# Second half of the gated values taken ahead of the last weight units, in the tail of an expert item

## The chip, the cores and the metric

The kernel runs on one core of a Trainium2 chip. The metric is device microseconds (us) for one execution of the whole kernel, as the median of several runs. Engines: PE is TensorE (matmuls and transposes), PEld its weight loads, DVE is VectorE, ACT is ScalarE, POOL is GpSimd, SP is SyncE, which issues the weight transfers.

## The reference, cut to what matters

The layer mixes a short convolution, differential attention and memory attention for 1024 tokens of width 1024, and then runs a mixture of 32 experts of which each token takes 4. Only the experts' part matters here:

```
def expert_block(args):
    tok, g, e = args
    xb = h_pad[tok]
    gu = xb @ w_gate_up[e] + b_gate_up[e]
    gate, up = jnp.split(gu, 2, axis=-1)
    gate = jnp.minimum(gate, SWIGLU_LIMIT)
    up = jnp.clip(up, -SWIGLU_LIMIT, SWIGLU_LIMIT)
    act = (up + 1.0) * (gate * jax.nn.sigmoid(SWIGLU_ALPHA * gate))
    y = act @ w_down[e] + b_down[e]
    return y * g[:, None].astype(y.dtype)
```

## The kernel before

**Items.** The experts' part is a loop over items. An item is one expert with up to 256 of its tokens, in one or two blocks of up to 128. A second block of at most 64 tokens is "short". An item with one block is called single here, one with two double. `by_size` picks the variant of the code by the item's own size, and `size_next` tells whether a next item follows and whether it is double.

**Units.** Each item takes 12 weight units of 1 MB (128 x 2048 floats), numbered u0 to u11: u0 to u3 gate and up for the first 512 columns (c = 0), u4 to u7 the same for the second 512 (c = 1), u8 to u11 the down projection: u8 and u9 with the first half of the gated values a, u10 and u11 with the second half. PE needs a high part and a low part of every operand, since a product is made of three: high x high, high x low, low x high. ACT makes the high part of a unit (`high_unit`, line 1150: a rounding copy), DVE the low part (`low_unit`, line 1564: original minus high). There are four places for high parts, so unit u is rounded once PE has used unit u - 4, and for the first units of the next item this reaches over the end of the item: unit 1 of the next item waits for u9, unit 2 for u10.

**Activations.** The gated values of half c are made on DVE (`products`), turned by PE (`turn_a`, transposes on line 922), rounded by ACT (`a_high`, line 1198) and subtracted by DVE (`a_low`, line 1585). u10 and u11 wait for `a_low` of half 1. The rows of the next item take the same way: `turn_x(b)` on PE (line 915) for block b, `x_high(b)` on ACT (line 1160), `x_low(b)` on DVE (line 1575). Both blocks are turned through the same PSUM banks, so `turn_x(1)`, which exists only before a double item, waits until `x_low(0)` has read them. u0 of the next item waits for `x_low` of all its blocks.

**Results.** ACT copies the down products out (`results`, line 1211, and line 1213 for the lower rows of a short block); for a short block DVE adds and scales (lines 1592 and 1632). Each half of the result raises `y_made`. The second block of the next item's u0 writes a PSUM bank that these results are read from, so in a double item its bias matmul waits for `y_made`:

```
if (len(kinds), b, c) in ((2, 1, 0), (1, 0, 1)):
    pe.wait_ge(s["y_made"], it * 2 + 1)
```

**Order.** Every engine works through its own instructions in the order in which `item` writes them for that engine; nothing reorders them. Across engines there are only semaphores. The order of the tail, from u8 on, is what the change edits.

Of the kernel before, what the change touches and what calls it, by code (L numbers as in the profile page):

```python
# [52 lines left out]
SLOTS = 12  # L53
# [33 lines left out]
def hymba_kernel(nc, a, out):  # L87
    ctx = ExitStack()
    with ctx:
# [596 lines left out]
        def _(pe):  # L686
# [19 lines left out]
            for g in range(NG):  # L706
                u, kind, x, half = groups[g]
# [217 lines left out]
            def use_unit(it, u, kinds):  # L925

                side, c, half = UNITS[u]
                high = w_high_part(u).rearrange("p (k n) -> p k n", k=4)
                low = w_low_part(u).rearrange("p (k n) -> p k n", k=4)
                rows = a_split if side == "d" else x_split  # L930
                pe.wait_ge(s["w_low_made"], it * 12 + (u + 1))
                if side == "d":
                    pe.wait_ge(s["a_low"], it * 2 + (half + 1))
                elif u == 0:
                    for b in range(len(kinds)):
                        pe.wait_ge(s_xlow[b], it + 1)
                    pe.wait_ge(s["picked"], it + 1)
                for b, kind in enumerate(kinds):
                    bank = ps[:, out_bank(side, c, b, kinds), :]
                    if half == 0:  # L940
                        if side == "d":
                            if b == 0:
                                pe.wait_ge(s["y_made"], it * 2 + 1)
                            else:
                                pe.wait_ge(s["silu_made"] if c == 0 else s["up_read"], it * 2 + 3)
                        else:
                            pe.wait_ge(s["silu_made"] if side == "g" else s["up_read"], it * 2 + (c + 1 if len(kinds) > 1 else 1))
                            if (len(kinds), b, c) in ((2, 1, 0), (1, 0, 1)):
                                pe.wait_ge(s["y_made"], it * 2 + 1)
                        which = 1 if side == "d" else 0  # L950
                        row = picked[:, which, 0:P] if kind == "full" else picked[:, which, SHORT:SHORT + P]
                        at = (D if side == "u" else 0) + HALF * c
                        mm(bank, row, mem_r[:, at:at + HALF], True, False)
                    for kk in range(4):
                        k = 4 * half + kk
                        first, second = rows[:, k, b, 0, :], rows[:, k, b, 1, :]
                        mm(bank, first, high[:, kk, :], False, False)
                        last = mm(bank, first, low[:, kk, :], False, kind == "short" and k == KD - 1)
                        if kind == "full":
                            last = mm(bank, second, high[:, kk, :], False, k == KD - 1)  # L960
                last.then_inc(s["w_used"], 1)

            def item(it, size_next, kinds):
                for u in range(6):
                    use_unit(it, u, kinds)

                pe.wait_ge(s["a_made"], it * 2 + 2)
                for b in range(len(kinds)):
                    pe.wait_ge(s_xlow[b], it + 1)
                turn_a(0, kinds)  # L970
                for u in range(6, 8):
                    use_unit(it, u, kinds)
                with pe.If(size_next > 0):
                    pe.wait_ge(s_gather[0], it * 16 + 32)
                    pe.wait_ge(s["a_low"], it * 2 + 1)
                    turn_x(0)
                use_unit(it, 8, kinds)
                pe.wait_ge(s["a_made"], it * 2 + 3)
                turn_a(1, kinds)
                use_unit(it, 9, kinds)  # L980
                with pe.If(size_next > P + 1):
                    pe.wait_ge(s_gather[1], it * 16 + 32)
                    pe.wait_ge(s_xlow[0], it + 2)
                    turn_x(1)
                with pe.Else():
                    pe.sem_inc(s_xturned[1], 1)
                for u in range(10, SLOTS):
                    use_unit(it, u, kinds)

            for b in range(BLOCKS):  # L990
                pe.wait_ge(s_gather[b], 16)
# [4 lines left out]
            with pe.Fori(0, MAX_ITEMS // GROUP) as group:  # L996
                size_group = pe.value_load(table[2:3, bass.ds(group * GROUP + 1, 1)], min_val=0, max_val=CAP + 1)
                with pe.If(size_group > 0):
                    with pe.Fori(0, GROUP) as place_in:
                        it = group * GROUP + place_in  # L1000
# [8 lines left out]
        def _(act):  # L1009
# [136 lines left out]
            def high_unit(it, u):  # L1146

                act.wait_ge(s_w[home(u)], arrived(u, it))
                act.wait_ge(s["w_used"], it * 12 + (u + 1))
                act.activation(w_high_part(u), ring[:, home(u), :], ACT.Copy).then_inc(s["w_high_made"], 1)  # L1150
# [20 lines left out]
            def up_rest(it, c, kinds):  # L1171
                if "short" in kinds:
                    b = kinds.index("short")
                    act.wait_ge(s["w_used"], it * 12 + (HI_SLOTS + 4 * c + 4))
                    act.wait_ge(s["a_turned"], it * 2 + (c + 1))
                    act.activation(up_b[0:SHORT, b, :], ps[SHORT:P, out_bank("u", c, b, kinds), :], ACT.Copy).then_inc(s["rest_made"], 1)
# [39 lines left out]
            def item(it, size_next, kinds):  # L1216
                high_unit(it, 3)
                high_unit(it, 4)
                gate_rest(it, 0, kinds)
                high_unit(it, 5)  # L1220
                sigmoids(it, 0, kinds)
                high_unit(it, 6)
                up_rest(it, 0, kinds)
                high_unit(it, 7)
                gate_rest(it, 1, kinds)
                sigmoids(it, 1, kinds)
                a_high(it, 0, kinds)
                high_unit(it, 8)
                high_unit(it, 9)
                up_rest(it, 1, kinds)  # L1230
                with act.If(size_next > 0):
                    x_high(0, it + 1, "full")
                high_unit(it, 10)
                high_unit(it, 11)
                a_high(it, 1, kinds)
                with act.If(size_next > 0):
                    high_unit(it + 1, 0)
                    expert = act.value_load(table[0:1, bass.ds(it + 2, 1)], min_val=0, max_val=EXPERTS - 1)
                    act.wait_ge(s["w_used"], it * 12 + (HI_SLOTS + 10))
                    pick_expert(bass.ds(expert, 1))  # L1240
                    by_second(act, size_next, lambda kind: x_high(1, it + 1, kind), lambda: act.sem_inc(s_xhigh[1], 1))
                    high_unit(it + 1, 1)
                    high_unit(it + 1, 2)
                for c in range(2):
                    results(it, c, kinds)
                if "short" not in kinds:
                    act.sem_inc(s["rest_made"], 6)
# [34 lines left out]
        def _(dve):  # L1282
# [278 lines left out]
            def low_unit(it, u):  # L1561

                dve.wait_ge(s["w_high_made"], it * 12 + (u + 1))
                dve.tensor_tensor(w_low_part(u), ring[:, home(u), :], w_high_part(u).bitcast(f32), ALU.subtract)\  # L1564
                    .then_inc(s["w_low_made"], 1)
# [68 lines left out]
            def item(it, size_next, kinds):  # L1634
                low_unit(it, 3)
                gates(it, 0, kinds)
                low_unit(it, 4)
                low_unit(it, 5)
                products(it, 0, kinds)
                low_unit(it, 6)  # L1640
                low_unit(it, 7)
                gates(it, 1, kinds)
                a_low(it, 0, kinds)
                low_unit(it, 8)
                products(it, 1, kinds)
                low_unit(it, 9)
                with dve.If(size_next > 0):
                    x_low(0, it + 1, "full")
                with dve.Else():
                    dve.sem_inc(s_xlow[0], 1)  # L1650
                low_unit(it, 10)
                a_low(it, 1, kinds)
                low_unit(it, 11)
                with dve.If(size_next > 0):
                    low_unit(it + 1, 0)
                    by_second(dve, size_next, lambda kind: x_low(1, it + 1, kind), lambda: dve.sem_inc(s_xlow[1], 1))
                    low_unit(it + 1, 1)
                    low_unit(it + 1, 2)
                for c in range(2):
                    results(it, c, kinds)  # L1660
                if "short" not in kinds:
                    dve.sem_inc(s["sum_made"], 6)
                dve.sem_inc(s["dve_item"], 1)
# [52 lines left out]
```

## Time and profile before

| what | value |
|---|---|
| median of 3 runs | 2270.81 us (2268.62 to 2271.24) |
| the profiled execution, its own time | 2271.15 us |
| its span, first to last instruction | 2269.5 us |
| PE busy | 2156.5 us, 95% of the span |
| DVE, ACT, POOL busy | 69%, 59%, 15% of the span |
| DMA, mean | 237 GB/s |

Rows of the timeline give the start in us from the span's start, the length in us, the engine and line, the names, how many instructions were merged, and in brackets the idle time of the engine before it with what ended it. Items run from 572.8 us to 2234 us of the span.

### The profile page before, as it was taken

To read this page: it belongs to the slowest core of one execution; us is meant where nothing else is said; L and a number is where in the kernel's file an instruction comes from. 1 tells how busy PE (TensorE), PEld (TensorE's weight loads), DVE (VectorE), ACT (ScalarE), POOL (GpSimd) and SP (SyncE) were. 2 spreads that over 40 slices of the span, in tenths; PEclk is the share of its full clock that TensorE was granted. 3 is DMA by queue.
4 is the path that set the end of the run, shared out by engine and by line. 5 is a ranking of instruction groups with operands and counts; after the bars stand their busy time and mean duration, and the time that the engine had idled before them with its cause. 6 is when DMAs were issued, how large, how long until landed. Compare 5 with 4: busy or idle time off the path is not lost.

```text
span 2269.5 us, 34559 instructions
## 1 busy us (share of the span) xinstructions
PE 2156.5 (95%) x10770; PEld 1790.6 (79%) x10771; DVE 1557.7 (69%) x1641; ACT 1331.5 (59%) x1524; POOL 340.2 (15%) x306
## 2 busy tenths in 40 slices
PE   7999999895999999999999999999999999999993
PEld 6889767895778888877887878788888878888882
DVE  4411289566577577589758989886677897767764
ACT  5111179443565466577657777775555777556654
POOL 1000000023111022022112121221210122111200
PEclk9999989997999999999999999999999999999997
DMA  5111300434787689599869999996676999677854
GB/s 198 57 56 38 111 1 1 183 106 132 260 292 237 207 294 344 192 365 376 306 206 372 371 368 359 371 343 232 222 234 226 355 373 333 228 232 240 306 162 171
DMA packets 265277, 536.75 MB, mean 237 GB/s; under 512 B 14478, under 2 KB 31144, under 8 KB 265132
## 3 DMA queue, kind: packets, MB, share of 16 engines
q1 hardware_dynamic: 248332, 488.26, 60.3%
q0 software_dynamic: 16896, 47.83, 8.6%
q8 instruction: 32, 0.52, 0.1%
q14 instruction: 17, 0.14, 0.0%
HBM read 499.29 MB, written 36.75 MB: 236 GB/s over the span
## 4 chain that ended last, share of the span: by engine, by line
PE 83%; issue 6%; DVE 5%; ACT 3%; DMA 1%; POOL 0%; DVEq 0%; SPq 0%; ACTq 0%; POOLq 0%
PE ps L688 79%; PE ps L915 1%; ACT hT_hi L1150 1%; PE ps L922 1%; DVE hT_lo L1575 1%; DVE w_lo L1564 1%; PE ps L825 1%; ACT region_mem L1185 0%; DVE work L1615 0%; DVE hT_lo L1585 0%; DMA weight_ring<-in_w_mix_in 0%; ACT hT_lo L1198 0%; DVE weight_ring L1691 0%; DVE work L1393 0%; DVE m_max L1355 0%
## 5 line engine op out<-in xcount | busy, mean ns | idle before, releaser
L688 PE MATMUL ps<-hT_hi,hT_lo 128*128 128x512 f32 (+1 forms) x4304 | 1396.4, 388 | 13.2 <-DVE hT_lo L1585 12.3
L688 PEld LDWEIGHTS ps<-hT_hi,hT_lo 128*128 128x128 f32 x4304 | 806.7, 188 | 182.4 <-DVE w_lo L1564 18.2
L1150 ACT ACTIVATE hT_hi<-weight_ring 128x2048 fp32r<-128x2048 f32 x417 | 786.1, 1914 | 174.8 <-PE ps L688 118.4
L1564 DVE TENSOR_TENSOR slots_between<-weight_ring,hT_hi 128x2048 fp32r<-128x2048 f32 x245 | 552.5, 2286 | 129.5 <-ACT hT_hi L1150 128.9
L688 PE MATMUL ps<-slots_between,hT_lo 128*128 128x512 f32 x1344 | 525.7, 391 | 0.0
L1564 DVE TENSOR_TENSOR w_lo<-weight_ring,hT_hi 128x2048 fp32r<-128x2048 f32 x140 | 319.8, 2285 | 33.6 <-ACT hT_hi L1150 33.6
L688 PE MATMUL ps<-w_lo,hT_lo 128*128 128x512 f32 (+1 forms) x896 | 336.0, 375 | 0.0
L688 PEld LDWEIGHTS ps<-slots_between,hT_lo 128*128 128x128 f32 x1344 | 253.4, 189 | 53.9
L688 PEld LDWEIGHTS ps<-w_lo,hT_lo 128*128 128x128 f32 x896 | 168.7, 188 | 30.3
L609 POOL DMA_INDIRECT residual_rows<-work,idx_now x48 | 121.8, 2537 | 469.5 <-ACT work L1211 274.9
L603 POOL DMA_INDIRECT work<-normed_rows,idx_far x49 | 86.2, 1759 | 442.1 <-PE ps L915 269.8
L688 PE MATMUL ps<-mem_there,picked 128*128 128x512 f32 x288 | 123.5, 429 | 8.8 <-issue 5.9
L1585 DVE TENSOR_TENSOR hT_lo<-ps,hT_lo 128x512 fp32r<-128x512 f32 x96 | 58.9, 636 | 99.1 <-ACT hT_lo L1198 99.1
L1185 ACT ACTIVATE region_mem<-ps,limits 128x512 f32<-128x512 f32 x78 | 52.3, 681 | 123.1 <-PE ps L688 122.6
L688 PE MATMUL ps<-hT_hi,w_hi 128*128 128x512 f32 x256 | 101.1, 395 | 7.5 <-DVE hT_lo L1309 7.5
L589 POOL DMA_INDIRECT expert_lists<-pay,dest_i x32 | 32.6, 1020 | 497.2 <-DVE dest_i L1494 489.9
L1592 DVE TENSOR_TENSOR work<-ps,work 64x512 f32<-64x512 f32 x54 | 36.8, 682 | 101.1 <-ACT work L1169 54.4
L688 PE MATMUL ps<-hT_lo,w_hi 128*128 128x512 f32 x256 | 100.4, 392 | 0.0
L688 PE MATMUL ps<-hT_hi,w_lo 128*128 128x512 f32 x256 | 100.4, 392 | 0.0
L1334 DVE COPY weight_ring<-ps 128x512 f32<-128x512 f32 x18 | 12.4, 691 | 124.5 <-PE ps L688 124.5
L1160 ACT ACTIVATE hT_lo<-ps 128x512 fp32r<-128x512 f32 (+1 forms) x96 | 48.3, 556 | 69.2 <-PE ps L915 69.2
L688 PE MATMUL ps<-last_slot,hT_lo 128*128 128x512 f32 (+1 forms) x256 | 87.2, 364 | 0.0
(251 smaller groups left out, 2418.6 us busy)
## 6 DMA issues: line engine op xcount, KB each, us to landing
weight_ring<-in_w_gate_up SPq DMA_DIRECT2D x280, 1024.0 KB, 7.8
weight_ring<-in_w_down SPq DMA_DIRECT2D x140, 1024.0 KB, 6.3
weight_ring<-in_w_mix_in SPq DMA_DIRECT2D x10, 1024.0 KB, 5.8
weight_ring<-in_x SPq DMA_DIRECT2D x8, 512.0 KB, 8.1
weight_ring<-in_w_mix_out SPq DMA_DIRECT2D x4, 1024.0 KB, 5.3
work<-in_x SPq DMA_DIRECT2D x8, 512.0 KB, 4.6
residual_rows<-work SPq DMA_DIRECT2D x8, 512.0 KB, 3.3
normed_rows<-work SPq DMA_DIRECT2D x8, 512.0 KB, 3.6
```

What stands on the lines that cost most here:

```text
L589: pool.indirect_dma_start(list_d[:, :], bass.IndirectOffsetOnAxis(ap=dest_i[:, i, c:c + 1], axis=0), pay[:, i, c, :], None).then_inc(s["li ...
L603: pool.indirect_dma_start(xg[rows, b, :], None, h_d[:, :], bass.IndirectOffsetOnAxis(ap=idx_far.bitcast(i32)[rows, b, 0:1], axis=0)).then_ ...
L609: pool.indirect_dma_start(acc_d[:, :], bass.IndirectOffsetOnAxis(ap=idx_now.bitcast(i32)[rows, b, 0:1], axis=0), y_rows[rows, b, :], None, ...
L688: return pe.matmul(o, l, r, start=first, stop=last)
L825: last = pe.transpose(ps[:, 4 + b // 4, P * (b % 4):P * (b % 4) + P], wk[:, 2 * (n % 2), P * b:P * b + P], ident[:, :])
L915: last = pe.transpose(ps[:, bank + half, P * k:P * k + P], xg[:, b, HALF * half + P * k:HALF * half + P * k + P], ident[:, :])
L1150: act.activation(w_high_part(u), ring[:, home(u), :], ACT.Copy).then_inc(s["w_high_made"], 1)
L1160: ins = act.activation(x_split[:, 4 * half:4 * half + 4, b, 0, cols], ps[:, bank + half, :].rearrange("p (k t) -> p k t", t=P)[:, :, cols] ...
L1185: ins = act.activation(sig_b[rows, b, :], gate_b[rows, b, :] if kind == "short" else ps[:, out_bank("g", c, b, kinds), :], ACT.Relu, scale ...
L1564: dve.tensor_tensor(w_low_part(u), ring[:, home(u), :], w_high_part(u).bitcast(f32), ALU.subtract)\
L1585: ins = dve.tensor_tensor(low_place(a_split[:, ks, b], kind), ps[:, turn_bank(c, b), :].rearrange("p (k t) -> p k t", t=P)[:, :, cols], a_ ...
L1592: dve.tensor_tensor(place, ps[0:SHORT, bank, :], place, ALU.add).then_inc(s["sum_made"], 1)
```

## The change

In `item`, for each of the three engines, the second half of the gated values comes ahead of the last weight units' parts. DVE: `a_low` of half 1 goes from between u10 and u11 to ahead of u10, and `x_low(0)` from ahead of u10 to behind u11. ACT: the high part of u10 goes ahead of `x_high(0)`, and `a_high` of half 1 ahead of the high part of u11. PE: u10 goes ahead of `turn_x(1)`.

```
-                for u in range(10, SLOTS):
-                    use_unit(it, u, kinds)
+                use_unit(it, 11, kinds)
...
                 use_unit(it, 9, kinds)
+                use_unit(it, 10, kinds)
                 with pe.If(size_next > P + 1):
                     pe.wait_ge(s_gather[1], it * 16 + 32)
                     pe.wait_ge(s_xlow[0], it + 2)
                     turn_x(1)
...
                 up_rest(it, 1, kinds)
+                high_unit(it, 10)
                 with act.If(size_next > 0):
                     x_high(0, it + 1, "full")
-                high_unit(it, 10)
+                a_high(it, 1, kinds)
                 high_unit(it, 11)
-                a_high(it, 1, kinds)
...
                 low_unit(it, 9)
+                a_low(it, 1, kinds)
+                low_unit(it, 10)
+                low_unit(it, 11)
                 with dve.If(size_next > 0):
                     x_low(0, it + 1, "full")
                 with dve.Else():
                     dve.sem_inc(s_xlow[0], 1)
-                low_unit(it, 10)
-                a_low(it, 1, kinds)
-                low_unit(it, 11)
```

The order on DVE in the tail of an item with a short second block, before. Line 1564 is a unit's low part (u9, then u10, then u11), line 1575 is `x_low(0)`, line 1585 `a_low` of half 1:

```order
L1564 TENSOR_TENSOR w_lo<-weight_ring,hT_hi 128x2048 [waits w_high_made]
L1647 COMPARE_AND_BRANCH
L1571 REGISTER_ALU
L1575 TENSOR_TENSOR hT_lo<-ps,hT_lo 128x4x128 [waits x_high0]
L1575 TENSOR_TENSOR hT_lo<-ps,hT_lo 128x4x128
L1647 UNCONDITIONAL_BRANCH
L1649 UNCONDITIONAL_BRANCH
L1563 REGISTER_ALU
L1564 TENSOR_TENSOR w_lo<-weight_ring,hT_hi 128x2048 [waits w_high_made]
L1585 TENSOR_TENSOR hT_lo<-ps,hT_lo 128x4x128 [waits a_high]
L1585 TENSOR_TENSOR hT_lo<-ps,hT_lo 128x4x64
L1564 TENSOR_TENSOR w_lo<-weight_ring,hT_hi 128x2048 [waits w_high_made]
```

The same place of the changed kernel:

```order
L1564 TENSOR_TENSOR w_lo<-weight_ring,hT_hi 128x2048 [waits w_high_made]
L1585 TENSOR_TENSOR hT_lo<-ps,hT_lo 128x4x128 [waits a_high]
L1585 TENSOR_TENSOR hT_lo<-ps,hT_lo 128x4x64
L1563 REGISTER_ALU
L1564 TENSOR_TENSOR w_lo<-weight_ring,hT_hi 128x2048 [waits w_high_made] x2
L1650 COMPARE_AND_BRANCH
L1571 REGISTER_ALU
L1575 TENSOR_TENSOR hT_lo<-ps,hT_lo 128x4x128 [waits x_high0]
L1575 TENSOR_TENSOR hT_lo<-ps,hT_lo 128x4x128
```

`a_low` now stands directly behind u9's low part and waits there for ACT; both low parts of u10 and u11 stand ahead of `x_low(0)`.

On PE, the end of the same variant in the changed kernel, from the branch behind u10 to the first matmul of u11 (line 915 is `turn_x(1)`; before the change these rows stood ahead of u10):

```order
L982 COMPARE_AND_BRANCH
L983 ISA
L984 REGISTER_ALU [waits gathered1]
L915 MATMUL ps<-ident,work 128x128 [waits x_low0]
L915 MATMUL ps<-ident,work 128x128 x7
L982 UNCONDITIONAL_BRANCH
L986 UNCONDITIONAL_BRANCH
L931 REGISTER_ALU
L688 MATMUL ps<-hT_hi,hT_lo 128x512 [waits a_low,w_low_made]
```

The eight transposes moved behind the whole of u10, with u11 queued behind their wait for `x_low(0)`.

## Rows read from the trace of the kernel before

**Rows 1.** The page, busy time of each engine (share of the span), instructions:

```profile
PE 2156.5 (95%) x10770; PEld 1790.6 (79%) x10771; DVE 1557.7 (69%) x1641; ACT 1331.5 (59%) x1524; POOL 340.2 (15%) x306
```

**Rows 2.** Waits of 570 to 2235 us (total, times, longest), then that window's sums:

```profile
PE ps L688 <- DVE hT_lo L1585: 12.3, 15, 0.9
PEld ps L688 <- DVE w_lo L1564: 21.3, 28, 1.2
570.00:2235.00 1665.00, 1642.38 (x7523) 1348.82 (x7521) 1256.15 (x968) 1079.12 (x965) 290.79 (x239) 1.00 0.84 287
```

**Rows 3.** Counts by line over the whole span:

```profile
L1153 ACT ACTIVATE picked<-pick x35: 409/417/422, 558.9 to 2187.4; 128x256 fp32r x34, 128x256 fp32r<-128x256 f32 x1
L1198 ACT ACTIVATE hT_lo<-ps x96: 362/579/604, 608.1 to 2225.2; 128x512 fp32r<-128x512 f32 x78, 128x256 fp32r<-128x256 f32 x18
L1656 DVEq EVENT_SEMAPHORE  x22: 21/21/21, 625.2 to 2184.5; - x22
```

**Rows 4.** Timeline of DVE, tail of a single item ahead of a single one:

```profile
1240.10 2.28 DVE L1564 TENSOR_TENSOR w_lo<-weight_ring,hT_hi 128x2048 fp32r<-128x2048 f32 x1
1242.30 1.28 DVE L1575 TENSOR_TENSOR hT_lo<-ps,hT_lo 128x512 fp32r<-128x512 f32 x2
...
1245.70 0.68 DVE L1585 TENSOR_TENSOR hT_lo<-ps,hT_lo 128x512 fp32r<-128x512 f32 x1
...
1248.50 6.69 DVE L1564 TENSOR_TENSOR slots_between<-weight_ring,hT_hi 128x2048 fp32r<-128x2048 f32 x3
```

**Rows 5.** Timeline of ACT, the same tail:

```profile
1239.13 1.09 ACT L1160 ACTIVATE hT_lo<-ps 128x512 fp32r<-128x512 f32 x2 [1.40 <-PE ps L915]
1240.10 3.72 ACT L1150 ACTIVATE hT_hi<-weight_ring 128x2048 fp32r<-128x2048 f32 x2
1243.71 0.60 ACT L1198 ACTIVATE hT_lo<-ps 128x512 fp32r<-128x512 f32 x1
```

**Rows 6.** Timeline of PE, the same tail, to the next item's first matmul:

```profile
1241.90 0.60 PE L922 MATMUL ps<-ident,work 128*128 128x128 f32 x4
...
1246.53 0.47 PE L688 MATMUL ps<-hT_hi,hT_lo 128*128 128x512 f32 x1 [0.81 <-DVE hT_lo L1585]
...
1252.08 0.39 PE L688 MATMUL ps<-mem_there,picked 128*128 128x512 f32 x1
```

**Rows 7.** Timeline of PE, a single item ahead of a double one:

```profile
1099.97 1.03 PE L915 MATMUL ps<-ident,work 128*128 128x128 f32 x8
1100.93 0.47 PE L688 MATMUL ps<-hT_hi,hT_lo 128*128 128x512 f32 x1
```

**Rows 8.** Timeline of PE, ACT and DVE, a short double ahead of another:

```profile
1626.31 1.04 PE L915 MATMUL ps<-ident,work 128*128 128x128 f32 x8
1639.26 0.40 PE L688 MATMUL ps<-mem_there,picked 128*128 128x512 f32 x1
1627.38 0.66 ACT L1160 ACTIVATE hT_lo<-ps 128x256 fp32r<-128x256 f32 x2 [0.37 <-PE ps L915]
1631.96 1.92 ACT L1150 ACTIVATE hT_hi<-weight_ring 128x2048 fp32r<-128x2048 f32 x1 [2.12 <-PE ps L688]
1633.91 2.29 DVE L1564 TENSOR_TENSOR slots_between<-weight_ring,hT_hi 128x2048 fp32r<-128x2048 f32 x1 [1.74 <-ACT hT_hi L1150]
1636.12 0.68 DVE L1592 TENSOR_TENSOR work<-ps,work 64x512 f32<-64x512 f32 x1
1638.55 0.48 DVE L1632 TENSOR_SCALAR work<-work,idx_now 64x512 f32<-64x512 f32 x1
```

**Rows 9.** Windows at a long idle of PE (length, busy of PE, PEld, DVE, ACT, POOL with counts, PE clock, DMA share, GB/s):

```profile
636.00:639.00 3.00, 0.00 (x0) 0.00 (x1) 1.98 (x4) 1.83 (x3) 0.00 (x0) 0.89 0.55 165
639.00:642.00 3.00, 3.00 (x7) 2.43 (x8) 1.22 (x1) 1.37 (x1) 1.64 (x1) 0.50 0.83 231
645.00:650.00 5.00, 5.00 (x23) 4.04 (x23) 2.47 (x2) 3.97 (x3) 1.45 (x1) 0.99 0.78 238
```

More of the change, by code:

```diff
@@ L980, in item @@
                 use_unit(it, 9, kinds)
+                use_unit(it, 10, kinds)
                 with pe.If(size_next > P + 1):
@@ L986, in item @@
                     pe.sem_inc(s_xturned[1], 1)
-                for u in range(10, SLOTS):
-                    use_unit(it, u, kinds)
+                use_unit(it, 11, kinds)
             for b in range(BLOCKS):
@@ L1230, in item @@
                 up_rest(it, 1, kinds)
+                high_unit(it, 10)
                 with act.If(size_next > 0):
                     x_high(0, it + 1, "full")
-                high_unit(it, 10)
+                a_high(it, 1, kinds)
                 high_unit(it, 11)
-                a_high(it, 1, kinds)
                 with act.If(size_next > 0):
@@ L1646, in item @@
                 low_unit(it, 9)
+                a_low(it, 1, kinds)
+                low_unit(it, 10)
+                low_unit(it, 11)
                 with dve.If(size_next > 0):
@@ L1650, in item @@
                     dve.sem_inc(s_xlow[0], 1)
-                low_unit(it, 10)
-                a_low(it, 1, kinds)
-                low_unit(it, 11)
                 with dve.If(size_next > 0):
```

## The prediction

> **What bounds the kernel now.** I read the page first: PE is busy 95% of the span, no other engine above 69% [rows 1]. Then the sums of the experts' part: PE is busy 1642.38 of 1665.00 us there, so all its idle time together is 22.6 us [rows 2]. The waits say what it is: 12.3 us in 15 waits of up to 0.9 us end with `a_low` (line 1585) [rows 2]. That is the only wait which this change can take away, so no gain above 12.3 us is to be had. (The waits of PEld for line 1564, 21.3 us in 28, are weight loads that came late while matmuls were still running; the 22.6 us hold all that was lost.) So PE bounds the experts' part by its own work, and the question is less what the change removes than whether it puts a new wait on PE.
>
> For that I followed the tails of the items in the timeline, and counted them by kind. There are 35 items (one `picked` each) and 96 `a_high`, two for each item and two more for each double one: 96 = 70 + 26, so 13 double items and 22 single; 18 of the 96 are narrow, so 9 double items are short [rows 3]. The branch "next is not double" is taken 22 times [rows 3]. Of 34 boundaries 12 so lead into a double item. The 15 waits fall one on each boundary from single to single; that leaves 7 double to single, 6 double to double (all after a short item, one of them into a full one) and 6 single to double.
>
> **Single to single, 15 times: a gain.** Before, DVE goes low(u9), `x_low(0)`, low(u10), `a_low`, low(u11) without a pause, and `a_low` ends at 1245.70 + 0.68 = 1246.38; PE starts u10 at 1246.53, 0.15 later, having idled 0.81 [rows 4, 6]. After: ACT is free 1.40 before 1239.13, at 1237.73, and rounds u10 first (1.9), then `x_high(0)` until about 1240.6. Then it waits for the turned values, which end at 1241.90 + 0.60 = 1242.50 [rows 5, 6], and `a_high` ends at 1243.15 (0.60 from its row, 0.05 to react). DVE, free at 1240.10 + 2.28 = 1242.38, now waits 0.8 for it, and `a_low` ends at 1243.85. But u10 also needs its low part, which now stands behind `a_low`: one in a run of three takes 6.69 / 3, a pitch of 2.20 [rows 4], so it ends at 1246.05. PE starts u10 at 1246.20 in place of 1246.53. So 0.33 is gained and not 0.81: the stall goes from `a_low` to low(u10). The bounds: 0 if something on the way is 0.3 late, 0.81 if low(u10) were ready.
>
> What comes behind: low(u11) ends at 1248.25, `x_low(0)` (1.28) at 1249.5, low of the next item's u0 at 1251.65, and PE wants to start that item at 1252.08 - 0.33 = 1251.75 [rows 4, 6]. It just fits; if it is late, nothing of the 0.33 arrives. I take 15 x 0.33 = -5.0 us, with bounds 0 and -12.2.
>
> **Single to double, 6 times: a loss.** Before, `turn_x(1)` runs in the very time in which PE would wait: 1099.97, with u10 following at 1100.93 and no idle [rows 7]. A unit takes (1252.08 - 1246.53) / 2 = 2.78 [rows 6], so u11 begins near 1103.7. After, that cover is gone. Low(u10) is ready at 1100.46 (the same DVE chain as above, moved by 145.6), PE begins u10 at 1100.6 and is through at 1103.4. Now `turn_x(1)` has to wait for `x_low(0)`, which stands behind low(u11): 1100.46 + 2.20 + 1.28 = 1103.94. The transposes take 0.96 [rows 7], and u11 begins at 1104.95. That is 1.25 us later. Queued behind it: `x_high(1)` on ACT, then the high parts of two units, then the results that the next item's second block waits for. From the turn's end at 1105.0: 1.0, two pitches of 1.82 (3.72 for two in a row, less the overlap [rows 5]) and two results of 0.6 end at about 1110.9. The bias matmul is due 13 matmuls of 0.227 and the unit u11 after 1104.95, at 1110.7 to 1110.85. So 0.2 more is lost where the next item's second block is full, and nothing where it is short and `x_high(1)` 0.43 quicker [rows 8]. One of the four full double items follows a double one, so 3 of the 6 pay it. The bounds are 0.8 (the stalls a bit shorter) and 2.0 (the results 0.75 late). Sum: 6 x 1.25 + 3 x 0.2 = +8.1 us.
>
> **Double to double, 6 times: the largest term.** Here PE is not waiting for `a_low`, so nothing is gained, and the turn itself is in time. But it is moved past u10, which has 20 matmuls of 5.00 / 22 = 0.227 each (23 in the last window, one of them cut at its edge) [rows 9]: the turn ends 4.54 later, at 1627.35 + 4.54 = 1631.89 [rows 8]. On ACT, `x_high(1)` begins there instead of at 1627.38, and the next item's high(u1) and high(u2) stand behind it. High(u2) began at 1631.96 before, as soon as u10 had freed its place, and ACT had idled 2.12 ahead of it [rows 8]. That slack is less than the shift. Now: 1631.92 + 0.54 + 1.82 = 1634.28, ending at 1636.20. DVE: low(u1) starts at 1634.4, low(u2) at 1636.6 where it was 1633.91 [rows 8], and ends at 1638.9. Behind it stand the additions and scalings of the two halves. Before, they began at 1636.12, waited for the second half, and ended at 1638.55 + 0.48 = 1639.03 [rows 8]. Now nothing of theirs is still being waited for, and 0.68 + 0.48 twice with small hand-overs is 2.35: they end at 1641.2. The bias matmul of the next item's second block waits for exactly this. It stood at 1639.26 [rows 8], with 0.23 to spare; now it starts at 1641.35. Stall 2.1; in the one that leads into a full item `x_high(1)` is 0.43 longer, stall 2.5. Sum: 5 x 2.1 + 2.5 = +13.0 us. Bounds for one: 1.5 (ACT and DVE overlap better than my pitches) and 2.7.
>
> **Double to single, 7 times, and the last item: nothing.** There is no `turn_x(1)`. DVE pays for the wait at `a_low`, but a double item's u8 to u11 take 4.5 us or more each on PE against 2.2 on DVE, which covers it. The price without that cover would be the 0.8 of the wait.
>
> DMAs: no issue moves on SP, and the weights' arrival is set by units used, which shift by the stalls alone. POOL's gather of the second block starts later by the shift of `turn_x(1)`, and is wanted an item later. Its scatter waits for `y_made`, and slips by up to 2 us with it; what waits for that comes at the end of the next item.
>
> **The sum.** Made against the profiled execution: 2271.15 - 5.0 + 8.1 + 13.0 = 2287.25 us. The median is 0.34 lower than that execution, so I say 2287.
>
> **Rivals.**
> (a) The clock falls in the new stalls. After PE's idle of 3.00 us at 636 to 639 the granted clock went to 0.50, and PE did 7 matmuls in 3 us where full speed has 23 in 5 [rows 9]. Half speed lasted until about 645, so that one fall cost 3 us beside the stall. The 0.81 stalls brought none. The new ones of 2.1 and 2.5 lie between, nearer to the one that did. Each fall would add 3: one gives 2290, all six 2305. The Trainium skill ("TensorE: Matmul & The Clock Gate", HAM oscillation) says that idle pauses between bursts of matmuls send the clock back to half, with a penalty of half the time spent there. By that rule the pauses here are rather too short, and the sum stays; the fall at 636 us agrees with its direction.
> (b) Faster: `a_low` is the one that counts and `x_low(0)` isn't late. It needs `x_low(0)` to end before u10 does, that is DVE's chain to be 0.6 shorter than I have it in the single to double tail, and the results of double items not to be held by high(u2). For it speaks that the 12.3 us are `a_low`'s by name [rows 2]; against it that DVE has no pause between 1240.10 and 1255.19 to make up anything [rows 4]. At -12.2: 2259; with 0.33 each: 2266.
> (c) The double to double term is hidden (the results' add on DVE slips ahead of the bias matmul after all): -5.0 + 8.1 gives 2274, no measurable change. The 0.23 to spare against a shift of 2.2 speaks against it.
>
> **Chances.** A run can tell about 0.2% (4.5 us) from no change. The sum as it stands, 2280 to 2290: 0.76. (a), 2290 to 2305: 0.14. (c) 0.05. (b) 0.04; the rest goes to losses that I haven't seen. Slower by over 0.2% therefore 0.91, within it 0.05, faster 0.04. The range: below, the lower bounds of the two losses (6 x 0.8 + 6 x 1.5 = 13.8) with -5.0 give 2280, and with half of the untaken gain 2276; above, three falls of the clock give 2296. I give 2277 to 2297, which leaves out the four or more falls, (b) and (c).
>
> **What would show each step.** Right: the waits of PE for line 1585 are gone or a few tenths, and about 15 waits of 0.4 to 0.5 us for line 1564 stand in their place; about 6 waits of 0.5 of line 915 for `x_low(0)`, line 1575; and 6 waits of about 2 us of a bias matmul for line 1632, each at the start of an item after a short one. The double items that follow one another get 2 us longer (61 to 63), the singles ahead of singles 0.3 shorter (37.2 to 36.9). Wrong: no wait of PE for line 1632, or windows behind such waits with a clock under 1.

## The result and the profile after

The changed kernel takes 2296.07 us in the median (2295.38 to 2299.24) against 2270.55 before. That is 25.5 us slower; the ratio, estimated over all the runs and not from the two medians alone, is 1.0116, with a 95% interval of 1.0100 to 1.0132. The forecast was 2287, with 2277 to 2297 as the range. The profiled execution took 2296.72 us.

The engines' busy times on the page of the changed kernel:

```profile
PE 2170.6 (95%) x10770; PEld 1792.1 (78%) x10771; DVE 1561.2 (68%) x1641; ACT 1331.9 (58%) x1524; POOL 336.1 (15%) x306
```

Against [rows 1] nothing was added and nothing taken away: the counts are the same, and of the busy times PE's is clearly longer, by 14.1 us; the others moved by 4.1 or less. The waits of PE in the experts' part of the changed kernel (engine, line, what it waited for, total us, times, longest), and the sums of that stretch (columns as in [rows 9]):

```profile
PE ps L688 <- DVE work L1632: 11.2, 6, 2.3
PE ps L688 <- DVE w_lo L1564: 9.5, 22, 0.5
PE ps L688 <- issue: 8.0, 13, 2.9
PE ps L688 <- DVE hT_lo L1575: 2.3, 1, 2.3
PE ps L915 <- DVE hT_lo L1575: 2.2, 6, 0.4
570.00:2260.00 1690.00, 1655.71 (x7522) 1349.59 (x7520) 1259.59 (x968) 1078.46 (x965) 287.12 (x239) 0.99 0.83 282
```

The 12.3 us for `a_low` (line 1585) of [rows 2] are gone. Three waits stand in their place: 9.5 us for a unit's low part, 2.2 us of the transposes for `x_low(0)`, and 11.2 us of bias matmuls for the results (line 1632). All of PE's idle time is 1690.00 - 1655.71 = 34.3 us, where it was 22.6. The mean clock of the stretch reads 0.99 where it was 1.00.

The idle time grew by only 11.7 us and the kernel by 25.5. Two things are not in it. One is the clock, below. The other is that the ends of matmuls are modelled: a row of one lasts 0.39 us, while in a dense run the next one begins 0.23 after it. So a break costs about 0.16 more than its idle time shows (the stall of 1.88 below puts the first two bias matmuls of its item 5.00 apart where they were 2.96, which is 2.04), and these waits of PE are 48 where they were 24. Hand-overs still shorter than 0.16 show as no idle time at all.

**Single to single.** The tail that answers to [rows 4] to [rows 6], in the changed kernel. DVE, then ACT, then PE:

```profile
1245.13 2.28 DVE L1564 TENSOR_TENSOR w_lo<-weight_ring,hT_hi 128x2048 fp32r<-128x2048 f32 x1
1248.24 0.69 DVE L1585 TENSOR_TENSOR hT_lo<-ps,hT_lo 128x512 fp32r<-128x512 f32 x1 [0.83 <-ACT hT_lo L1198]
1248.85 4.48 DVE L1564 TENSOR_TENSOR w_lo<-weight_ring,hT_hi 128x2048 fp32r<-128x2048 f32 x2
1253.25 1.28 DVE L1575 TENSOR_TENSOR hT_lo<-ps,hT_lo 128x512 fp32r<-128x512 f32 x2
1254.45 6.69 DVE L1564 TENSOR_TENSOR slots_between<-weight_ring,hT_hi 128x2048 fp32r<-128x2048 f32 x3
...
1247.61 0.60 ACT L1198 ACTIVATE hT_lo<-ps 128x512 fp32r<-128x512 f32 x1 [2.06 <-PE ps L922]
...
1251.18 0.50 PE L688 MATMUL ps<-hT_hi,hT_lo 128*128 128x512 f32 x1 [0.45 <-DVE w_lo L1564]
...
1257.07 0.49 PE L688 MATMUL ps<-mem_there,picked 128*128 128x512 f32 x1 [0.15 <-issue]
```

DVE waits 0.83 for `a_high`, and low(u10) comes out of the merged row two later, at 1248.85 + 2.28 = 1251.13; PE idles 0.45 for it where it idled 0.81 for `a_low`. That is the step that was forecast, at 0.48. The last row is the next item's first matmul: 0.15 of idle time that wasn't there before.

**Single to double.** PE in the tail that answers to [rows 7]:

```profile
1104.07 0.50 PE L688 MATMUL ps<-hT_hi,hT_lo 128*128 128x512 f32 x1 [0.41 <-DVE w_lo L1564]
...
1107.47 1.09 PE L915 MATMUL ps<-ident,work 128*128 128x128 f32 x8 [0.39 <-DVE hT_lo L1575]
```

Where the transposes filled the time ahead of u10, u10 now idles 0.41, and the transposes 0.39 behind it for `x_low(0)`.

**Double to double.** PE, ACT and DVE of a short double item ahead of another, as in [rows 8]:

```profile
1575.99 1.03 PE L915 MATMUL ps<-ident,work 128*128 128x128 f32 x8
...
1586.41 0.47 PE L688 MATMUL ps<-mem_there,picked 128*128 128x512 f32 x1 [1.88 <-DVE work L1632]
...
1577.06 0.66 ACT L1160 ACTIVATE hT_lo<-ps 128x256 fp32r<-128x256 f32 x2 [4.91 <-PE ps L915]
1577.60 3.73 ACT L1150 ACTIVATE hT_hi<-weight_ring 128x2048 fp32r<-128x2048 f32 x2
...
1579.56 4.50 DVE L1564 TENSOR_TENSOR slots_between<-weight_ring,hT_hi 128x2048 fp32r<-128x2048 f32 x2 [1.05 <-ACT hT_hi L1150]
1583.97 0.68 DVE L1592 TENSOR_TENSOR work<-ps,work 64x512 f32<-64x512 f32 x1
...
1585.79 0.48 DVE L1632 TENSOR_SCALAR work<-work,idx_now 64x512 f32<-64x512 f32 x1
```

The turn ends at 1577.02, and from there one follows the other without slack: `x_high(1)`, two high parts in one go, two low parts in one go, the additions, the scaling that ends at 1586.27, and 0.14 later the bias matmul, which had idled 1.88. Before, ACT had 2.12 and DVE 1.74 of idle time inside this chain [rows 8].

**The clock.** Windows around that stall (columns as in [rows 9]):

```profile
1584.60:1587.60 3.00, 1.19 (x5) 1.04 (x6) 1.60 (x4) 1.34 (x1) 0.49 (x1) 1.00 0.51 197
1587.60:1591.00 3.40, 3.40 (x9) 2.67 (x9) 2.29 (x1) 1.37 (x1) 1.13 (x1) 0.50 0.55 64
1591.00:1594.40 3.40, 3.40 (x16) 2.80 (x16) 0.00 (x0) 0.55 (x1) 0.04 (x1) 1.00 0.93 261
```

After the stall the granted clock fell from 2.4 GHz to 1.2 GHz for 3.4 us, in which PE did 9 matmuls where 16 fit at full clock. That costs half of 3.4, 1.7 us. Apart from half clock at the entry of the experts' part and the fall at 639 us, which the kernel before has too, the trace has four falls, at 1587.6, 1652.4, 1990.4 and 2055.2 us. Each stands behind one of the six stalls for line 1632, and these four stalls are of 1.88 us. The other two, of 2.31 us at 745.1 and of 1.36 us at 1715.8, brought none; the longest stall is not among those with a fall.

**Where the 25.5 us are.** From the times at which PE finished the last unit of each item, the two traces differ as follows (profiled executions, us; what a stall at the start of an item costs counts with the boundary ahead of it, except for single to single):

| boundary | times | forecast | in the trace |
|---|---|---|---|
| single to single | 15 | -5.0 | -1.3 |
| single to double | 6 | +8.1 | +7.8 (+9.5 but for the clock, below) |
| double to double | 6 | +13.0 | +19.1, of it four falls of the clock 6.8 |
| the rest | 8 | 0 | -0.2 |
| sum | | +16.1 | +25.4 |

One of the six single to double boundaries hides something. Its item starts behind the long idle of [rows 9]. Half clock lasted until 645 us there before; in the changed kernel's execution it was over sooner, as the clock column of these two windows shows, so that this item got back 1.7 us by the clock alone:

```profile
638.70:642.10 3.40, 3.40 (x9) 2.63 (x9) 1.72 (x1) 1.26 (x1) 1.64 (x1) 0.50 0.83 210
642.10:645.50 3.40, 3.40 (x16) 2.77 (x16) 0.80 (x2) 1.92 (x1) 0.00 (x0) 1.00 0.89 163
```

### The profile page after: what moved, and what is told of

The parts are those of the page before. It is cut to its first block, busy times and chain, and to the rows that moved or that the text cites. A ratio compares the mean times of both kernels' runs of the same rounds, so it can differ in the third digit from the quotient of the medians.

```text
span 2295.1 us, 34559 instructions
## 1 busy us (share of the span) xinstructions
PE 2170.6 (95%) x10770; PEld 1792.1 (78%) x10771; DVE 1561.2 (68%) x1641; ACT 1331.9 (58%) x1524; POOL 336.1 (15%) x306
## 4 chain that ended last, share of the span: by engine, by line
PE 84%; DVE 7%; issue 4%; ACT 2%; DMA 1%; POOL 0%; SPq 0%; DVEq 0%; ACTq 0%; POOLq 0%
PE ps L688 79%; DVE w_lo L1564 2%; PE ps L915 2%; PE ps L922 2%; DVE slots_between L1564 1%; ACT hT_hi L1150 1%; PE ps L825 1%; ACT hT_lo L1198 1%; DVE hT_lo L1575 0%; DMA weight_ring<-in_w_mix_in 0%; DVE weight_ring L1691 0%; DVE work L1592 0%; DVE work L1393 0%; DVE m_max L1355 0%; POOL expert_lists L589 0%
## 5 line engine op out<-in xcount | busy, mean ns | idle before, releaser
L609 POOL DMA_INDIRECT residual_rows<-work,idx_now x48 | 97.1, 2023 | 378.3 <-ACT work L1211 207.9
L688 PE MATMUL ps<-mem_there,picked 128*128 128x512 f32 x288 | 125.2, 435 | 21.9 <-DVE work L1632 11.2
L1198 ACT ACTIVATE hT_lo<-ps 128x512 fp32r<-128x512 f32 x96 | 50.0, 549 | 97.6 <-PE ps L922 97.6
```

The lines of the kernel that those rows point to most:

```text
L609: pool.indirect_dma_start(acc_d[:, :], bass.IndirectOffsetOnAxis(ap=idx_now.bitcast(i32)[rows, b, 0:1], axis=0), y_rows[rows, b, :], None, ...
L688: return pe.matmul(o, l, r, start=first, stop=last)
L1198: ins = act.activation(a_split[:, 4 * c:4 * c + 4, b, 0, cols], ps[:, turn_bank(c, b), :].rearrange("p (k t) -> p k t", t=P)[:, :, cols], ...
```

## The experiments

Each run has its own runs of the kernel before on the same chip, and the ratios are to those.

**PE's order alone.** The kernel before with the edit on PE only:

```
                 use_unit(it, 9, kinds)
+                use_unit(it, 10, kinds)
                 with pe.If(size_next > P + 1):
...
                     turn_x(1)
...
-                for u in range(10, SLOTS):
-                    use_unit(it, u, kinds)
+                use_unit(it, 11, kinds)
```

> The kernel before with only the change on PE: u10 ahead of turn_x(1); ACT and DVE as before. My theory (the late turn of the second block is what costs): single to single 0; single to double 6 x 1.1, since u10 waits 0.8 for a_low and the turn no longer fills that time; double to double as in the changed kernel, about +19 in six with the falls of the clock. Sum +26: about 2296 us, as slow as the whole change. Rival (the order on ACT and DVE is what costs): about 2271 us.

Measured: 2297.55 us (2290.95 to 2300.33) against 2272.04, ratio 1.0120 (1.0103 to 1.0136). The move on PE alone costs what the whole change costs. Its waits:

```profile
PE ps L688 <- DVE hT_lo L1585: 17.3, 21, 0.8
PE ps L688 <- DVE work L1632: 11.2, 6, 2.3
```

The 15 waits for `a_low` have become 21: the six single to double tails, which `turn_x(1)` used to cover, have joined them. The waits for line 1632 are there to the tenth, with ACT and DVE in the order of before, so it is the late turn that makes them. This run also shows what a fall of the clock costs, since the same stall was followed by a fall at one place and by none at another. Two bias matmuls with the same stall, and the window behind each:

```profile
1584.46 0.47 PE L688 MATMUL ps<-mem_there,picked 128*128 128x512 f32 x1 [1.88 <-DVE work L1632]
1984.60 0.47 PE L688 MATMUL ps<-mem_there,picked 128*128 128x512 f32 x1 [1.88 <-DVE work L1632]
1584.60:1588.00 3.40, 3.40 (x16) 2.77 (x17) 1.28 (x1) 1.19 (x1) 1.62 (x1) 1.00 0.29 29
1985.40:1988.80 3.40, 3.40 (x10) 2.63 (x9) 1.93 (x1) 0.66 (x1) 1.53 (x1) 0.50 0.44 54
```

The item with the stall alone became 2.1 us longer than before, the one with the fall behind it 3.7. This profiled execution has two such falls and took 2290.95 us. Its other three runs took 2296.26 to 2300.33; they have no traces, but their mean granted clock is on record, 0.972 to 0.974 against 0.978, so more of their time was at half clock.

**ACT's and DVE's order alone.** The changed kernel with PE's order put back (the diff above, reversed, on the changed kernel).

> The changed kernel with PE's order put back (turn_x(1) ahead of u10). My theory: turn_x(1) now waits for an x_low(0) that stands behind low(u11): 3.8 in each of 6 single to double tails, 2.7 in each of 6 double to double, nothing gained single to single. Sum +39: about 2310 us, with falls of the clock up to 2320. The bias matmul's wait for the results of a short item (line 1632) is gone, since PE itself is late. Rival (PE's move is the only cost): about 2266 to 2271 us.

Measured: 2328.73 us (2326.24 to 2330.18), ratio 1.0249 (1.0232 to 1.0266). It is 19 us slower than the forecast of 2310, and 9 slower than the 2320 that the forecast allowed with falls of the clock. The direction is as forecast. Its largest wait of PE:

```profile
PE ps L915 <- DVE hT_lo L1575: 38.4, 12, 3.9
```

These are the 39 us of the forecast, 12 times as counted. The rest is the clock, of which I had allowed too little: after 600 us the trace has 12 stretches at half clock in the experts' part, ten of 3.4 us and two of 6.8, 47.6 us together, where the kernel before has one of 6.8. Half of the difference is lost, 20.4 us. So PE's move belongs to the change: with `x_low(0)` behind low(u11), the turn can only be late.

**The next item's units ahead of its second block.** The changed kernel; only in double items (`len(kinds) > 1`) ACT and DVE do this, the single ones stay as they were:

```
+                    high_unit(it + 1, 1)
+                    high_unit(it + 1, 2)
                     by_second(act, size_next, lambda kind: x_high(1, it + 1, kind), ...)
-                    high_unit(it + 1, 1)
-                    high_unit(it + 1, 2)
...
+                    low_unit(it + 1, 1)
+                    low_unit(it + 1, 2)
                     by_second(dve, size_next, lambda kind: x_low(1, it + 1, kind), ...)
-                    low_unit(it + 1, 1)
-                    low_unit(it + 1, 2)
```

> The changed kernel; in double items alone the next item's high(u1), high(u2) and low(u1), low(u2) go ahead of x_high(1) and x_low(1). My theory: the results of a short item are held by the chain turn_x(1), x_high(1), high(u1), high(u2), low(u2); with the two units done before, the results end at about 63.2 us of the item against a bias matmul at 63.7, so the wait for line 1632 and the four falls of the clock go: -19, about 2277 us. Rival (the results are late for another reason, such as the two low parts ahead of x_low(0)): still about 2296 us.

Measured: 2280.00 us (2278.12 to 2282.96) against 2272.04, ratio 1.0043 (1.0026 to 1.0059). This chip's kernel before is 1.5 us slower than that of the first comparison, so it is about 17.5 us off the changed kernel. All its waits of PE (lines 1564 and 1575 are 1568 and 1579 here):

```profile
PE ps L688 <- DVE w_lo L1568: 9.3, 22, 0.5
PE ps L688 <- issue: 6.6, 9, 2.5
PE ps L688 <- DVE hT_lo L1579: 2.4, 1, 2.4
PE ps L915 <- DVE hT_lo L1579: 2.2, 6, 0.4
```

The wait for the results is gone, and this execution has no fall of the clock between 570 us and the end of the last item. The one at 639 us, which both kernels have and which has nothing to do with this chain, is missing too, and this execution is the fastest of the four (2278.12). The chain through `x_high(1)`, high(u1), high(u2) and low(u2) was the cause of the six stalls for line 1632.

**Low(u10) ahead of `a_low`.** The changed kernel with two lines of DVE swapped:

```
                 low_unit(it, 9)
-                a_low(it, 1, kinds)
                 low_unit(it, 10)
+                a_low(it, 1, kinds)
                 low_unit(it, 11)
```

> The changed kernel with low(u10) ahead of a_low on DVE. My theory: DVE's wait of 0.8 us for a_high makes u10's low part late now and the next item's u0 late after; with low(u10) in that time, each of 15 single to single tails gets 0.8 shorter (12 us) and the 6 single to double ones 0.4: about 2282 us. Rival (a_low must come first for u10 to start early): 2296 us or slower.

Measured: 2280.53 us (2276.71 to 2282.25), ratio 1.0036 (1.0022 to 1.0050), about 17 us off the changed kernel. Its waits (left out are those at the entry of the experts' part, which every kernel has, and the idle time listed as issue):

```profile
...
PE ps L688 <- DVE work L1632: 11.0, 6, 2.3
...
PE ps L915 <- DVE hT_lo L1575: 1.3, 6, 0.2
PE ps L688 <- DVE w_lo L1564: 0.4, 1, 0.4
PE ps L688 <- DVE slots_between L1564: 0.3, 1, 0.3
```

The 22 waits for a low part have come down to 0.4 us in one and 0.3 in another. The single items in a row are 36.4 us long, against 37.2 before and 37.3 in the changed kernel. So the pause of 0.83 us on DVE did two things: it delayed low(u10), and at the end of the item low of the next u0. The six stalls for line 1632 are still there, with a fall of the clock behind three of them against four, so the gain isn't the clock's.

**`x_low(0)` third, on DVE alone.** With the two faults known, I looked for a version without them. The kernel before with:

```
                 low_unit(it, 9)
+                low_unit(it, 10)
+                a_low(it, 1, kinds)
                 with dve.If(size_next > 0):
                     x_low(0, it + 1, "full")
                 with dve.Else():
                     dve.sem_inc(s_xlow[0], 1)
-                low_unit(it, 10)
-                a_low(it, 1, kinds)
                 low_unit(it, 11)
```

> The kernel before with one edit, on DVE alone: x_low(0) goes behind low(u10) and a_low, ahead of low(u11). My theory: in 15 single to single tails the wait of 0.8 us goes (-12); in 6 single to double ones turn_x(1) now waits about 1 us for x_low(0) (+0.9 each, +5.4); double to double keeps its slack, since x_low(0) ends near 49.5 us of the item and the turn begins at 50.8. Sum about -6.6: 2265 us beside a before of 2271 to 2272. Rival (DVE is so full that low(u0) of the next item is late anyway): no change.

Measured: 2272.78 us (2270.39 to 2274.91) against 2271.62, ratio 1.0005 (0.9996 to 1.0014). A miss: no gain. Two of its waits:

```profile
PE ps L915 <- DVE hT_lo L1575: 3.7, 5, 0.8
PE ps L688 <- DVE w_lo L1564: 3.6, 16, 0.4
```

The first is the price that I had counted. The second I had not: low(u11) now stands behind `x_low(0)`, and u11 waits for it (15 of the 16; one of 0.4 in the last item is in the kernel before too).

**The same, chosen by the next item's size.** DVE takes the order of the last experiment only in a single item that no double one follows, and that of before elsewhere.

> The kernel before with DVE's order chosen by the sizes: in a single item that a single one or none follows, low(u10), a_low, x_low(0); elsewhere the order of before. My theory: the 12 us of line 1585 without the price: 2259 to 2260 us beside a before of 2271 to 2272. Rival (the branches, or DVE's fullness, eat it): 2265 us or more.

Measured: 2269.05 us (2267.57 to 2271.43), ratio 0.9990 (0.9981 to 0.9999). A miss again, 9 us above the forecast, and by the same step: its waits still hold this row, with the price for the transposes gone.

```profile
PE ps L688 <- DVE w_lo L1564: 3.6, 16, 0.4
```

In this run and in the one before it, four items also start with 1.25 us of idle time that the profile lists as issue, where the kernel before has 0.66. They are those items that begin a group of four (the loop over items is written in groups of four) and follow a single item. What makes that difference was not tried.

**Both repairs.** The changed kernel with low(u10) ahead of `a_low` and, in double items, the next item's units 1 and 2 ahead of its second block.

> The changed kernel with both repairs: low(u10) ahead of a_low, and in double items the next item's units 1 and 2 ahead of x_high(1) and x_low(1). My theory: the two add up, -16 and -17 from the changed kernel's 2297 on this chip: about 2264 us, so the move of the gated values is worth something once the two new waits are out. Rival (one repair takes up the slack of the other): 2275 us or more.

Measured: 2261.35 us (2260.62 to 2263.10) against 2271.62, ratio 0.9957 (0.9943 to 0.9970). They add up: 25.5 us slower than before has become 10.3 faster, 35.8 in all, where the two repairs alone gave 17.5 and 17. Here `x_low(0)` stands behind low(u11), which the two misses lacked; the next experiment tries just that.

**By the next item's size, with `x_low(0)` last.** The kernel before with one edit, on DVE:

```
                 low_unit(it, 9)
-                with dve.If(size_next > 0):
+                with dve.If(size_next > P + 1 if len(kinds) == 1 else size_next > 0):
                     x_low(0, it + 1, "full")
+                    low_unit(it, 10)
+                    a_low(it, 1, kinds)
+                    low_unit(it, 11)
                 with dve.Else():
-                    dve.sem_inc(s_xlow[0], 1)
-                low_unit(it, 10)
-                a_low(it, 1, kinds)
-                low_unit(it, 11)
+                    low_unit(it, 10)
+                    a_low(it, 1, kinds)
+                    low_unit(it, 11)
+                    with dve.If(size_next > 0):
+                        x_low(0, it + 1, "full")
+                    with dve.Else():
+                        dve.sem_inc(s_xlow[0], 1)
```

> The kernel before with one edit on DVE: in a single item that a single one or none follows, low(u10), a_low, low(u11), x_low(0); elsewhere the order of before. It differs from the run before last only in that x_low(0) stands behind low(u11). My theory, mended: what ate half of the gain there was low(u11), late by the 1.2 us of x_low(0) ahead of it. So the tails from single to single get 0.8 to 1.1 us shorter, as they did with both repairs (-14 in 15), and those to a double item cost nothing: about 2257 us beside a before of 2271.6. Rival (DVE has no time left in these items, whatever the order): 2266 us or more.

Measured: 2255.42 us (2254.73 to 2259.48) against 2270.27, ratio 0.9938 (0.9924 to 0.9952). It is 14.9 us faster than before and has the lowest ratio of all, though its interval overlaps that of both repairs (0.9943 to 0.9970). DVE in one of its single to single tails, and the sums of its experts' part:

```profile
1236.14 4.49 DVE L1564 TENSOR_TENSOR w_lo<-weight_ring,hT_hi 128x2048 fp32r<-128x2048 f32 x2
1240.54 0.68 DVE L1585 TENSOR_TENSOR hT_lo<-ps,hT_lo 128x512 fp32r<-128x512 f32 x1
1241.14 2.28 DVE L1564 TENSOR_TENSOR w_lo<-weight_ring,hT_hi 128x2048 fp32r<-128x2048 f32 x1
1243.34 1.28 DVE L1575 TENSOR_TENSOR hT_lo<-ps,hT_lo 128x512 fp32r<-128x512 f32 x2
1244.54 6.68 DVE L1564 TENSOR_TENSOR slots_between<-weight_ring,hT_hi 128x2048 fp32r<-128x2048 f32 x3
...
570.00:2225.00 1655.00, 1642.02 (x7529) 1350.18 (x7528) 1257.55 (x969) 1081.41 (x967) 304.86 (x240) 1.00 0.85 288
```

No pause on DVE, and PE's idle time is down to 13.0 us in the experts' part, from 22.6. (The profiled execution, 2258.27 us, is one of the slower ones, 12.9 faster than that of the kernel before.) ACT and PE have the order of before.

## Why the prediction was right, point by point

- **What bounds the kernel, and what there was to gain.** Right in the main. PE's own work stayed the bound, and the one wait that the change could take away was the 12.3 us for line 1585. It went. As an upper bound 12.3 was too tight, since a break costs more than its idle time shows: in the last experiment the 15 tails got 13.8 us shorter in the trace, 0.92 each where 0.81 of idle time stood.
- **Single to single, -5.0.** The step on u10 held: 0.45 of idle time in place of 0.81. The step that failed is the one that says "It just fits": in the changed kernel low of the next item's u0 ends at about 1254.45 + 2.29 = 1256.74, PE was due at about 1256.76 (the last matmul of u11 begins at 1256.53, and one takes 0.23), and it begins at 1257.07. The forecast left 0.1 us between the two, less than the 0.15 that it had itself read as the hand-over from DVE to PE, so "it just fits" did not follow even from its own rows; and the hand-over here took 0.3. Why it is longer here than at u10, no run shows. So about 0.3 of the 0.36 was given back at the start of the next item, and the term is -1.3 in place of -5.0. The forecast had named this case ("if it is late, nothing of the 0.33 arrives") but counted the full gain. By the items, six of the fifteen kept 0.30 to 0.41 us, the four that follow a double item and the two that begin behind 0.7 of idle time in both kernels; the other nine came out 0.01 to 0.16 longer. The swap of low(u10) and `a_low` shows it: without DVE's pause both waits go, and the items get 0.8 us shorter.
- **Single to double, +8.1.** Right within its bounds: 7.8 as it stands, 9.5 without the 1.7 that the clock gave back in one of them. The waits are the two that it worked out, and the 0.2 at the bias matmul of a full second block came as 0.15, too short to show as idle time.
- **Double to double, +13.0.** Right in mechanism and size: without the falls of the clock it is 19.1 - 6.8 = 12.3. PE's order alone makes it, and taking the next item's units out of the chain unmakes it. The slack that the forecast went by, 0.23 us at the bias matmul and 2.12 on ACT, was the right thing to read.
- **Rival (a), the clock.** I gave it 0.14, against 0.76 for the sum as it stands, and it came, with four falls in the profiled execution; it is over half of the difference between 2287 and 2296. Its size was wrong too: I took 3 us for a fall from a stretch of half clock that lasted twice as long, and the falls here cost 1.7 each. That the median still lies in the range is luck, by 0.9 us: the range left out four or more falls, and four at 3 us would have given 2299. Two errors, in their number and in their price, made up for one another. The Trainium skill ("TensorE: Matmul & The Clock Gate", HAM oscillation) puts the penalty at half of the time spent at half clock. The traces agree: of 3.4 us that is 1.7, and with PE's order alone the item with a fall grew by 1.6 more than the one without (3.7 against 2.1). My reading of that section, that pauses of 2 us are rather too short to bring the clock down, did not hold: 1.88 us of idle were followed by a fall in some places and not in others.
- **The signs.** Those of the waits came as named: none for line 1585, 22 for line 1564 (the 15, six more in the single to double tails, and the one in the last item that was there before), six of 0.4 for line 915, six of about 2 us for line 1632. Two did not fit. The single items in a row are 37.3 long and not 36.9. And four of the double items behind a double one grew by 3.7 to 3.8 us and not by 2, since a clock under 1, which the forecast had named as a sign of being wrong, stood behind four of the six waits for line 1632.
- **Rivals (b) and (c).** Both out. The 12.3 us were `a_low`'s by name, but taking `a_low` first isn't what frees them; the results' additions didn't slip ahead of anything.

The sum was 9 us low by two things of the same sign: 3.7 from the start of the single items, and the clock, 6.8 lost less 1.7 got back. The remaining terms were off by 1.4 and -0.7.

## What to carry to other kernels

A wait that the profile names shows which value came last, not that it has to be made first: here the value stood in an engine's queue behind work that could have filled the time, and what helped was to leave no pause on that engine. Before moving a step past another, read the slack at every place where its followers are waited for, the far ones too; a turn moved by 4.5 us had 0.23 us to spare four steps and one item later. And where the followers differ with the next item's size, let the order differ with it.

## What the runs showed of the hardware

The same idle time of TensorE, 1.88 us, was followed by 3.4 us at 1.2 GHz at one place and by none at another, in one execution (PE's order alone, windows above). In the changed kernel a longer one of 2.31 us was followed by none. So a stall of some 2 us costs between itself and itself plus 1.7 us, and executions of such a kernel can differ by that much for each stall. The spread fits: PE's order alone went from 2290.95 to 2300.33 us, with a mean granted clock of 0.978 in the fastest execution and 0.972 in the slowest, while the kernel before beside it went from 2269.38 to 2273.62 at 0.976 to 0.978. Which executions had how many falls was seen in the profiled ones alone.
